# Head sums of q and k on TensorE: one fp32 product of the squares, or two fp32r products of their high and low halves

## What is computed

```python
def rmsnorm(x, g):
    xf = x.astype(jnp.float32)
    y = xf * lax.rsqrt(jnp.mean(xf * xf, axis=-1, keepdims=True) + RMS_EPS)
    return (y * g.astype(jnp.float32)).astype(x.dtype)
...
for i in range(DEPTH):                      # DEPTH = 2
    xn = rmsnorm(h, norm_mix[i])
    proj = jnp.einsum('bsd,dn->bsn', xn, w_in[i])
    q, k, v, cb, cc, cu, pu, gate_logits = jnp.split(proj, splits, axis=-1)
    qh = rmsnorm(heads(q), q_norm[i])       # 8 heads of 64
    kh = rmsnorm(heads(k), k_norm[i])
    att = stick_breaking_attention(qh, kh, heads(v))
    conv = cb * causal_short_conv(cc * cu, conv_w[i])
    pool = causal_pool_mixer(pu, pool_w[i]) * pool_scale[i]
    ... gates, branch and output projections; a search over 16384 experts; a gated embedding
```

## Time and profile before

| | |
|---|---|
| median of 3 runs | 3908.99 us (3905.82 to 3909.05) |
| profiled execution, its own time | 3910.81 us |
| its span on the core | 3909.0 us |
| mean granted clock of TensorE | 0.992 of full |
| PE busy | 3828.8 us, 98% of the span |
| DVE busy | 2878.5 us, 74% |
| ACT busy | 1450.8 us, 37% |
| POOL busy | 1474.3 us, 38% |

### The profile page before, as it was taken

How to read it: one execution, slowest core, us unless ns; L and a number is a source line. 1 busy time by engine, 2 the same in 40 slices (tenths; PEclk the granted TensorE clock), 3 DMA queues, 4 the chain that set the end, 5 groups by cost and what they waited for, 6 DMA issues and landing times.

```text
span 3909.0 us, 53929 instructions
## 1 busy us (share of the span) xinstructions
PE 3828.8 (98%) x17258; PEld 3140.4 (80%) x17258; DVE 2878.5 (74%) x4061; ACT 1450.8 (37%) x1957; POOL 1474.3 (38%) x935
## 2 busy tenths in 40 slices
PE   8999999999999999999999999999999999999997
PEld 5777888888888878888767778888888887888886
DVE  6753658989997287788577536599899963888785
ACT  5533333333333333333444333333333333333334
POOL 1100003444444277666101000045444443777651
PEclk9999999999999999999999999999999999999998
DMA  3222223445554699999222223234455546999991
GB/s 114 70 86 97 92 92 123 144 172 189 187 188 175 209 357 360 358 352 342 102 69 77 85 93 101 88 131 145 172 194 192 189 165 231 370 361 352 351 330 70
DMA packets 323770, 740.36 MB, mean 189 GB/s; under 512 B 30497, under 2 KB 161697, under 8 KB 319905
## 3 DMA queue, kind: packets, MB, share of 16 engines
q1 hardware_dynamic: 104400, 381.73, 28.1%
q10 hardware_dynamic: 174160, 222.40, 16.6%
q0 software_dynamic: 45056, 134.38, 9.3%
HBM read 618.87 MB, written 119.54 MB: 189 GB/s over the span
## 4 chain that ended last, share of the span: by engine, by line
PE 95%; DVE 2%; issue 1%; ACT 1%; DMA 1%; POOL 0%; DVEq 0%; ACTq 0%; POOLq 0%; SPq 0%
PE banks L1218 62%; PE banks L1434 26%; PE banks L1413 2%; PE banks L1280 1%; PE banks L1270 1%; PE banks L1288 1%; PE banks L1360 0%; ACT hi L453 0%; PE banks L1265 0%; DVE xl L787 0%; DMA vrow<-in_stream,tail_v 0%; DVE lo L775 0%; DMA raw<-in_stream 0%; ACT xh L469 0%; DVE xl L956 0%
## 5 line engine op out<-in xcount | busy, mean ns | idle before, releaser
L1218 PE MATMUL banks<-xh,hi 128*128 128x512 f32 x3264 | 1293.1, 396 | 27.1 <-DVE xl L787 18.5
L1218 PE MATMUL banks<-xl,hi 128*128 128x512 f32 x3264 | 1276.0, 391 | 0.0
L1218 PE MATMUL banks<-xh,lo 128*128 128x512 f32 x3264 | 1273.7, 390 | 0.0
L401 POOL TENSOR_TENSOR lo<-raw,hi 128x1024 fp32r<-128x1024 f32 x240 | 646.0, 2692 | 984.0 <-ACT hi L453 983.8
L775 DVE TENSOR_TENSOR lo<-raw,hi 128x1024 fp32r<-128x1024 f32 x484 | 586.6, 1212 | 418.2 <-ACT hi L453 351.7
L453 ACT ACTIVATE hi<-raw 128x1024 fp32r<-128x1024 f32 x724 | 739.5, 1042 | 261.3 <-DMA raw<-in_stream 162.6
L1218 PEld LDWEIGHTS banks<-xh,hi 128*128 128x128 f32 x3264 | 615.4, 189 | 166.0 <-DVE xl L787 23.6
L1218 PEld LDWEIGHTS banks<-xh,lo 128*128 128x128 f32 x3264 | 614.6, 188 | 130.9
L1218 PEld LDWEIGHTS banks<-xl,hi 128*128 128x128 f32 x3264 | 616.0, 189 | 122.4 <-issue 5.6
L1434 PE MATMUL banks<-hi,ah 128*128 128x512 f32 x1536 | 475.2, 391 | 13.2 <-issue 11.7
L1434 PE MATMUL banks<-lo,ah 128*128 128x512 f32 x1536 | 474.4, 390 | 0.0
(11 more groups left out here) (211 smaller groups left out, 3442.0 us busy)
## 6 DMA issues: line engine op xcount, KB each, us to landing
raw<-in_stream SPq DMA_DIRECT2D x724, 512.0 KB
early<-eo ACTq DMA_DIRECT2D x256, 256.0 KB, 2.4
gate_table<-stage ACTq DMA_DIRECT2D x24, 2048.0 KB, 7.1
gb<-gate_table ACTq DMA_DIRECT2D x64, 768.0 KB
eb<-early ACTq DMA_DIRECT2D x64, 768.0 KB
hval<-early,tail_h POOLq DMA_INDIRECT x256
vrow<-in_stream,tail_v POOLq DMA_INDIRECT x256
hT<-in_xT ACTq DMA_DIRECT2D x2, 1024.0 KB, 8.1
```

The lines of the kernel that those rows point to most:

```text
L401: pool.tensor_tensor(lo[k % RING][:, :], raw[k % RAW][:, :], hi[k % RING][:, :].bitcast(f32), ALU.subtract).then_inc(lo_split, 1)
L1218: ins = pe.matmul(out_ap, st[slot][:, a:a + P], mv, start=first and i == 0, stop=last and i == 2)
```

## The change

The squares of q go to `qrs`, those of k to `ksq`. ACT then rounds each to an fp32r half (`qsh`, `ksh`), DVE subtracts it from the square to get the rest (`qsl`, `ksl`), and PE adds up two fp32r products in place of the one fp32 product, with `heads_r`, an fp32r copy of the ones matrix that ACT makes once at the start. Two counters are new: `qk_hi` (rounded) and `qk_lo` (rest ready), the latter being what PE waits for now. On ACT, squaring and rounding of k now stand ahead of the square root for q. On DVE, the split of weight 5 moves from between the two reciprocals to behind k's scaling.

```diff
@@ -155,6 +155,9 @@
     negones = sb("negones", o_c + 2048, [P, P])
     tri_r = sb("tri_r", o_c + 1536, [P, P], f32r)
     ones_r = sb("ones_r", o_c + 2048, [P, P], f32r)
+    heads_r = sb("heads_r", o_c + 1024, [P, P], f32r)
+    qsh, qsl = sb("qsh", o_r + 10 * KB, [P, SEQ], f32r), sb("qsl", o_r + 12 * KB, [P, SEQ], f32r)
+    ksh, ksl = sb("ksh", o_r + 5 * KB, [P, SEQ], f32r), sb("ksl", o_r + 7 * KB, [P, SEQ], f32r)
     iota = sb("iota", o_c + 2560, [P, NK])
     vt = sb("vt", o_c + 3072, [P, NVEC])
     tailcol = sb("tailcol", o_c + 3712, [P, 1])
@@ -280,6 +283,7 @@
         gate_scaled, ple_scaled, pj_out = sem("gate_scaled"), sem("ple_scaled"), sem("pj_out")
         ple_added = sem("ple_added")
 
+        qk_hi, qk_lo = sem("qk_hi"), sem("qk_lo")
         qk_sq, qk_ssq, qk_root, qk_ready = sem("qk_sq"), sem("qk_ssq"), sem("qk_root"), sem("qk_ready")
         v_turned, v_ready = sem("v_turned"), sem("v_ready")
         z_ready, abs_ready, ln_ready, sp_ready = sem("z_ready"), sem("abs_ready"), sem("ln_ready"), sem("sp_ready")
@@ -484,18 +488,23 @@
             act.wait_ge(const_ready, 1)
             act.activation(tri_r[:, :], negtri[:, :], ACT.Copy).then_inc(signs_ready, 1)
             act.activation(ones_r[:, :], negones[:, :], ACT.Copy).then_inc(signs_ready, 1)
+            act.activation(heads_r[:, :], headones[:, :], ACT.Copy).then_inc(signs_ready, 1)
             with act.Fori(0, DEPTH) as l:
                 root(l, 0)
                 with act.Fori(0, PAIRS) as b:
                     s2 = l * (2 * PAIRS) + b * 2
                     act.wait_ge(dve_evac, 4 + l * V_ALL + b * 8 + 1)
-                    act.activation(ksq[:, :], qb[:, :], ACT.Square).then_inc(qk_sq, 1)
+                    act.activation(qrs[:, :], qb[:, :], ACT.Square).then_inc(qk_sq, 1)
+                    act.wait_ge(qk_sq, s2 + 1)
+                    act.activation(qsh[:, :], qrs[:, :], ACT.Copy).then_inc(qk_hi, 1)
                     split(l, 4, b)
+                    act.wait_ge(dve_evac, 4 + l * V_ALL + b * 8 + 2)
+                    act.activation(ksq[:, :], kb[:, :], ACT.Square).then_inc(qk_sq, 1)
+                    act.wait_ge(qk_sq, s2 + 2)
+                    act.activation(ksh[:, :], ksq[:, :], ACT.Copy).then_inc(qk_hi, 1)
                     act.wait_ge(qk_ssq, s2 + 1)
                     act.activation(qrs[:, :], bank[2][:, :], ACT.Sqrt, bias=vt[:, C_QEPS:C_QEPS + 1])\
                        .then_inc(qk_root, 1)
-                    act.wait_ge(dve_evac, 4 + l * V_ALL + b * 8 + 2)
-                    act.activation(ksq[:, :], kb[:, :], ACT.Square).then_inc(qk_sq, 1)
                     split(l, 5, b)
                     act.wait_ge(qk_ssq, s2 + 2)
                     act.activation(ksq[:, :], bank[3][:, :], ACT.Sqrt, scale=1.0 / DH, bias=vt[:, C_EPS:C_EPS + 1])\
@@ -811,19 +820,23 @@
                     dve.wait_ge(tile_done, n0 + 1)
                     dve.tensor_tensor(qb[:, :], bank[0][:, :], rs[0][:, :], ALU.mult).then_inc(dve_evac, 1)
                     split(l, 4, b)
+                    dve.wait_ge(qk_hi, s1 * 2 + 1)
+                    dve.tensor_tensor(qsl[:, :], qrs[:, :], qsh[:, :].bitcast(f32), ALU.subtract).then_inc(qk_lo, 1)
                     dve.wait_ge(tile_done, n0 + 2)
                     dve.tensor_tensor(kb[:, :], bank[1][:, :], rs[0][:, :], ALU.mult).then_inc(dve_evac, 1)
+                    dve.wait_ge(qk_hi, s1 * 2 + 2)
+                    dve.tensor_tensor(ksl[:, :], ksq[:, :], ksh[:, :].bitcast(f32), ALU.subtract).then_inc(qk_lo, 1)
                     dve.wait_ge(qk_root, s1 * 2 + 1)
                     link(dve.reciprocal(qrs[:, :], qrs[:, :]))
                     dve.scalar_tensor_tensor(qb[:, :], qb[:, :], vt[:, bass.ds(l + C_QG, 1)], qrs[:, :],
                                              ALU.mult, ALU.mult).then_inc(qk_ready, 1)
-                    split(l, 5, b)
                     dve.wait_ge(tile_done, n0 + 3)
                     dve.tensor_tensor(vT[:, :], bank[4][:, :], rs[0][:, :], ALU.mult).then_inc(dve_evac, 1)
                     dve.wait_ge(qk_root, s1 * 2 + 2)
                     link(dve.reciprocal(ksq[:, :], ksq[:, :]))
                     dve.scalar_tensor_tensor(kb[:, :], kb[:, :], vt[:, bass.ds(l + C_KG, 1)], ksq[:, :],
                                              ALU.mult, ALU.mult).then_inc(qk_ready, 1)
+                    split(l, 5, b)
 
                     def softplus(h, meanwhile):
 
@@ -1261,8 +1274,9 @@
                               late=l * 3 if opening else None)
 
                     def ssq(z):
-                        pe.wait_ge(qk_sq, s1 * 2 + z + 1)
-                        pe.matmul(bank[2 + z][:, :], headones[:, :], ksq[:, :], start=True, stop=True).then_inc(qk_ssq, 1)
+                        pe.wait_ge(qk_lo, s1 * 2 + z + 1)
+                        pe.matmul(bank[2 + z][:, :], heads_r[:, :], (qsh, ksh)[z][:, :], start=True, stop=False)
+                        pe.matmul(bank[2 + z][:, :], heads_r[:, :], (qsl, ksl)[z][:, :], start=False, stop=True).then_inc(qk_ssq, 1)
 
                     def scores(h):
                         r = h * DH
```

## The result

The changed kernel takes **3945.42 us** (median of 5 runs, 3942.25 to 3946.34), against 3909.05 for the kernel before on the same chip (5 runs, 3905.82 to 3911.2). The ratio is 1.009, with a 95% interval of 1.0076 to 1.0103: slower by 0.9%. The prediction was 3919.3 with a range of 3914 to 3926. The direction was right, but 26 us are missing from the sum.

A forecast was written before the change was run, and what follows sets the result against it. PE was taken to bound the kernel, with 95% of the chain. Six steady pairs +3.9, layer 0's first pair +3.7 and layer 1's +2.7 gave +10.3 us on 3908.99: 3919.3 us, range 3914 to 3926.

The forecast's parts named there:

- The chain of the steady pair: Six steady pairs, k taken to first score: table load delays q's root; +0.65 us each, +3.9 us in all.
- A table switch costs more: Rival, ACT's table load ahead of q's root: costs twice its row, 1.28 us more per steady pair, 3929; chance 0.03.
- The head sums: On PE, two fp32r products take 0.46 us instead of 0.86, saving 0.40 us twice a pair.
- The fp32r products cost as much as the fp32 one: Rival, PE's head sums: no saving, only the first pairs pay 0.8 us each, 3921; chance 0.02.
- The first pairs: First pair of each layer, where PE waits for q's rest: +3.7 us in layer 0, +2.7 in layer 1.
- The wait for q's rest: PE idles ahead of q's head sum in the first pairs: 4.2 us in layer 0, 6.3 in layer 1.
- The moved split: DVE's split of weight 5, now behind k's scaling: gives 1.5 us back on the steady pair's chain.
- its cover: DVE's third read of scores waits for PE anyway, hiding weight 5's split; without that, 1.2 us per pair at most.
- The clock falls in every steady pair: Rival, PE's 1.4 us wait ahead of the scores: half clock costs 1.5 us times 6, 3928; chance 0.07.
- The selection: Picking of experts after attention in each layer, third turn: the prediction had no term for it, 0 us.
- What costs PE no time costs nothing: Whole kernel: PE holds 95% of the chain, so only work that costs PE time was counted.

The follow-up runs named there:

- Experiment 1: The changed kernel with the square root's table set loaded early on ACT, right behind the split of weight 4: 3924.03 us.
- experiment 8: The changed kernel with 12 tiny memsets ahead on DVE, q's root before k's squaring, rests subtracted earlier, k's head sum behind all of mix(2): 3905.01 us.
- experiment 3: The changed kernel with 12 tiny memsets ahead of everything on DVE: 3929.88 us.
- experiment 7: The changed kernel with 12 tiny memsets ahead on DVE and the split of weight 5 put back between the reciprocals: 3949.47 us.
- experiment 4: The changed kernel with the square root's table set loaded early on ACT and 12 tiny memsets ahead on DVE: 3912.11 us.
- experiment 5: The kernel before the change with 2 tiny memsets ahead of everything on DVE: 3922.75 us.

## Why the prediction was wrong

**The chain of the steady pair: right.** k taken to first score was worked out as 13.26 us and took 13.21; the way to the first score got longer by 0.63 us (the whole pair by 0.59), predicted 0.65. The table load lay where it was put, behind k's rounding, and took 1.28 us with q's root starting 0.02 behind it (100.89 + 1.28 = 102.17 against 102.19). The drain of about 1380 ns that the Trainium skill ("ScalarE: Activation LUTs", section "What ACT_TABLE_LOAD costs") adds to each load did not show here, neither behind the load nor ahead of it: the rounding of k ended at 100.88, and the load started at 100.89. Going by the row was right, and the rival "A table switch costs more" falls with it. Experiment 1 measured the load's worth on the path to the first score: at least 1.40 us a pair, the whole way from +0.63 to PE's own limit at -0.77.

**The head sums: right.** The chain of experiment 8 shows 0.23 us for each fp32r product, 0.46 for a sum. The rival "The fp32r products cost as much as the fp32 one" falls.

**The first pairs: right in kind, a size off.** Layer 0's cost 4.5 us where 3.7 was said; its upper bound, 4.6 for a longer stretch of half clock, holds it. The wait for q's rest was predicted at 4.2 us and is 4.20. Here it is in the timeline of PE, and the two products at line 1278 and 1279, 0.60 us apart instead of 0.23, show the half clock. I had put it down at 1.5 us, and this is the term that was sized wrong: from the restart at 40.06 to the first score at 54.88 PE took 14.8 us for work of 11.9, so the half clock cost 2.9:

```profile
40.06 0.79 PE L1278 MATMUL banks<-qsh,heads_r 128*128 128x512 f32 x1 [4.20 <-DVE qsl L824]
40.66 0.63 PE L1279 MATMUL banks<-qsl,heads_r 128*128 128x512 f32 x1
```

Layer 1's cost 2.4, predicted 2.7, with a wait of 5.8 us for 6.3. (The 6.3 does not follow from the prediction's own rows: PE's idle time begins at 1974.17 - 2.56 = 1971.61, and up to the restart at 1977.7 that is 6.1.)

**The moved split: right, and its cover held.** No product with `tri_r` waits in the trace after.

**The clock: wrong, 11.0 us.** The step that failed is the rival "The clock falls in every steady pair", which was given 0.07 on one piece of evidence: "at 1964.31 PE had waited 2.10 us and no clock fell". So the sum took the clock behind PE's new wait at nothing. A single wait that the clock survived says little about six others. In the trace after, waits of 1.4 us were followed by the half clock in five of six steady pairs; in experiment 3 in four of six; with waits of 2.6 us (experiment 7) in six of six; with no wait (experiments 1, 4 and 8) in none. So the wait is shown to be what brings the half clock on, though not every time. The price was too low as well: 1.5 us was read from one place, and the five cost 1.5, 3.2, 1.6, 3.2 and 1.6. The rival's 9 us stood close to the 11.0 that came; it had the mechanism and lacked the chance. The wait at 1964.31 itself was a poor witness. Every trace has it, 2.1 us ahead of the same product and some 6 us behind the wait before it. In six of the ten traces it was survived, and in four (experiments 1, 3, 5 and 7) the clock fell 1.2 to 1.3 us behind it. Here it is in experiment 3, with the clock of a stretch that follows:

```profile
1971.34 1.13 PE L1260 MATMUL banks<-sq,ones 128*128 128x512 f32 x2 [2.09 <-ACT sq L468]
```
```profile
1973.00:1975.00 2.00, 2.00 (x7) 1.54 (x6) 0.00 (x0) 1.87 (x2) 0.00 (x0) 0.50 0.03 8
```

So neither the length of a wait nor the work just ahead of it decides alone. Why one wait costs 0, another 1.5 and another 3.2 stays open.

**The selection: wrong, 12.5 us, and in no part of the prediction.** "What costs PE no time costs nothing" was right, but I took it to mean that where PE did not wait before, it would not wait after: everything outside the pairs was put at nothing without a look.
With both added, the sum would have been 10.7 + 11.0 + 12.5 = 34.2, against 31.5 measured (the rest is the -2.7 of the table), and the predicted range was too narrow mainly because it had no room for a loss outside the pairs.

## What to carry to other kernels

Where an engine goes from never waiting to a short wait in a place that repeats, price the wait and the clock that falls behind it: here 1.4 us of idle time brought 0.6 us of delay and up to 3.2 us of half clock. On ACT, order instructions so that a table load falls into a wait that exists anyway; moving that one load was worth 8 us of chain and all the half clock of the steady pairs. And before a change of a few microseconds is judged, shift an engine's code (here DVE's) by a few idle instructions: a kernel whose DVE and POOL contend near a small slack of PE can move by 13 us through nothing else, which here was more than the change itself was predicted to do.

## What the runs showed of the hardware

- Two instructions more at the start of DVE's program, computing nothing of use, made the kernel before 0.34% slower (3922.75 us against 3908.20); four made no difference; twelve made the changed kernel 15.5 us faster.
- A DVE CAST of 128x256 takes 0.29 us when it starts 0.12 us ahead of POOL's subtraction, and 2.42 us when it starts 0.14 us behind it. The 128x2048 products with two inputs take 2.29 and 4.2 to 4.4 us in the same way, while a reduction with one input beside POOL's subtraction kept its 2.29 us. Where DVE's product started first, POOL's subtraction took 3.80 us instead of 2.40.
- TensorE's granted clock fell to 0.50 behind waits of 1.4 us that interrupt a stream of dense products, in five places of six in one kernel and four of six in another. One wait of 2.1 us, the same in ten traces, was followed by the half clock in four of them.
